# Reordering the opening of a two-layer trunk kernel: rope steps, input copies, loads, and extra products on TensorE

## The reference, cut to what matters

```python
for l in range(DEPTH):
    h = rmsnorm(x, norm_g[l])
    proj = h @ w_in[l]
    (a_q, a_k, a_v, a_gate, b_u, b_v, b_gate,
     c_q, c_f, c_i, c_gate, merge) = jnp.split(proj, SPLIT_IDX, axis=-1)
    qa = rope(a_q.reshape(b_, s_, A_HEADS, A_HEAD_DIM), positions)
    ka = rope(a_k.reshape(b_, s_, A_KV_HEADS, A_HEAD_DIM), positions)
    out_a = sliding_window_attention(qa, ka, va, attn_sinks[l]) * jax.nn.silu(a_gate)
    ...
    y = jnp.sum(gates * mixed, axis=2) @ w_out[l]
    x = x + y
return rmsnorm(x, final_g)
```

## Time and profile before

| What | us |
|---|---|
| Median of 3 runs | 1032.23 |
| Lowest and highest run | 1032.17, 1032.27 |
| The profiled execution | 1032.96 |
| Its span on the core | 1031.1 |

### The profile page before, as it was taken

How to read it: one execution, slowest core, us unless ns; L and a number is a source line. 1 busy time by engine, 2 the same in 40 slices (tenths; PEclk the granted TensorE clock), 3 DMA queues, 4 the chain that set the end, 5 groups by cost and what they waited for, 6 DMA issues and landing times.

```text
span 1031.1 us, 15310 instructions
## 1 busy us (share of the span) xinstructions
PE 1013.6 (98%) x6388; PEld 854.8 (83%) x6388; DVE 640.6 (62%) x840; ACT 517.5 (50%) x804; POOL 287.8 (28%) x144
## 2 busy tenths in 40 slices
PE   7989999999999999999999999999999999999997
PEld 6869899888888888888888989988888888888876
DVE  6888865899543535445628689479983444444552
ACT  6855774766552332223456766577546233332333
POOL 1221113532421413233212111153243232322430
PEclk9989999999999999999999999999999999999999
DMA  6512221222123323224342222212232232323602
GB/s 219 154 63 82 84 68 57 82 82 83 62 63 102 111 90 106 82 82 129 117 133 82 83 83 84 63 61 83 83 102 61 82 103 82 102 84 100 203 2 81
DMA packets 93428, 94.71 MB, mean 92 GB/s; under 512 B 2272, under 2 KB 91568, under 8 KB 93360
## 3 DMA queue, kind: packets, MB, share of 16 engines
q1 hardware_dynamic: 93088, 93.60, 29.3%
q10 hardware_dynamic: 272, 0.14, 0.1%
HBM read 91.64 MB, written 2.10 MB: 91 GB/s over the span
## 4 chain that ended last, share of the span: by engine, by line
PE 93%; DVE 3%; ACT 1%; issue 1%; DMA 1%; ACTq 0%; DVEq 0%
PE pj L504 27%; PE pj L505 26%; PE pj L506 26%; PE mx L641 2%; PE mx L504 1%; PE mx L505 1%; PE mx L506 1%; PE mx L581 1%; PE mx L604 1%; PE mx L701 1%; PE mx L669 1%; PE mx L589 1%; DVE q_rot L1421 1%; PE mx L679 1%; PE mx L672 1%
## 5 line engine op out<-in xcount | busy, mean ns | idle before, releaser
L1161 POOL TENSOR_TENSOR w_lo<-w_raw,w_hi 128x1024 fp32r<-128x1024 f32 (+1 forms) x89 | 196.3, 2206 | 571.6 <-ACT w_hi L818 571.3
L504 PE MATMUL pj<-h_hi,w_hi 128*128 128x512 f32 x832 | 330.2, 397 | 0.0
L506 PE MATMUL pj<-h_hi,w_lo 128*128 128x512 f32 x832 | 324.6, 390 | 0.0
L505 PE MATMUL pj<-h_lo,w_hi 128*128 128x512 f32 x832 | 324.5, 390 | 0.0
L818 ACT ACTIVATE w_hi<-w_raw 128x1024 fp32r<-128x1024 f32 (+1 forms) x179 | 159.1, 938 | 161.3 <-PE pj L506 161.1
L1271 DVE TENSOR_TENSOR w_lo<-w_raw,w_hi 128x1024 fp32r<-128x1024 f32 (+1 forms) x90 | 161.3, 1792 | 70.7 <-ACT w_hi L818 70.4
L504 PEld LDWEIGHTS pj<-h_hi,w_hi 128*128 128x128 f32 x832 | 156.6, 188 | 34.7 <-issue 3.0
L506 PEld LDWEIGHTS pj<-h_hi,w_lo 128*128 128x128 f32 x832 | 156.5, 188 | 33.0
L505 PEld LDWEIGHTS pj<-h_lo,w_hi 128*128 128x128 f32 x832 | 156.7, 188 | 32.1 <-issue 1.0
L1385 DVE TENSOR_TENSOR merge_gate<-pj,rstd 128x512 f32<-128x512 f32 x48 | 33.2, 691 | 162.9 <-PE pj L506 162.9
L936 ACT ACTIVATE merge_gate<-merge_gate,small 128x512 f32<-128x512 f32 x48 | 34.3, 715 | 89.3 <-DVE merge_gate L1385 89.3
(11 more groups left out here) (257 smaller groups left out, 1497.6 us busy)
## 6 DMA issues: line engine op xcount, KB each, us to landing
w_raw<-in_w_in SPq DMA_DIRECT2D x61, 1024.0 KB, 5.5
w_raw<-in_w_branch SPq DMA_DIRECT2D x24, 512.0 KB, 3.4
w_raw<-in_w_out SPq DMA_DIRECT2D x6, 1024.0 KB, 5.2
x_tokens<-in_x SPq DMA_DIRECT2D x4, 512.0 KB, 6.6
w_raw_last<-in_w_out SPq DMA_DIRECT2D x2, 1024.0 KB, 7.7
sp_w_rows<-in_sp_w SPq DMA_DIRECT2D x2, 512.0 KB, 6.4
out<-out_low SPq DMA_DIRECT2D x4, 256.0 KB, 2.0
out<-out_high SPq DMA_DIRECT2D x4, 256.0 KB, 2.3
```

The costliest lines, as they stand in the source:

```text
L504: pe.matmul(bank, wh, ah, start=first, stop=False)
L505: pe.matmul(bank, wh, al, start=False, stop=False)
L506: return pe.matmul(bank, wl, ah, start=False, stop=final)
L1161: return pool.tensor_tensor(out=dst, in0=full, in1=hi.bitcast(f32), op=ALU.subtract)
```

## The change

It touches layer 0 alone, and seven places. The ropes of layer 0 move from phases 3, 4, 4, 5, 6 to 3, 3, 4, 4, 5, and `values_even` from phase 5 to phase 6. TensorE gets four 128 x 128 products of a matrix of ones ahead of the gains' transpose and five behind it. The constants are loaded by SP, as its first transfer, and no longer by ACT. SP loads unit 1 ahead of the positions. ACT makes the high parts of blocks 6 and 7 ahead of the plain copies of blocks 2 to 5, and copies in the order 5, 2, 3, then the high part of unit 1, then 4, 6, 7. TensorE waits for five copies instead of six ahead of job 2.

```diff
-ROPE_FIRST = (3, 4, 4, 5, 6)
+ROPE_FIRST = (3, 3, 4, 4, 5)
...
             buf, src = unit_load(0)
+            sp.dma_start(CST[:, :], consts[:, :]).then_inc(cst_in, 16)
             load_x(0)
...
             load_x(3)
+            load_weights(sp, 1)
             sp.dma_start(POSI[:, :], positions[0].partition_broadcast(P)).then_inc(pos_in, 16)
-            for v in range(1, RB):
-                load_weights(sp, v)
+            load_weights(sp, 2)
...
+            def warm(count):
+                for _ in range(count):
+                    pe.matmul(M[0][:, 0:P], ONE[:, :], ONE[:, :], start=True, stop=True)
+
+            pe.wait_ge(fill_done, 1)
+            warm(4)
             pe.wait_ge(cst_in, 16)
             pe.wait_ge(norm_in, 16)
             pe.transpose(M[1][:, 0:16], VN[0:16, :], CST[0:16, 0:16]).then_inc(normT_done, 1)
+            warm(5)
             transpose_x(0)
...
-                        pe.wait_ge(xT_evac, 6)
+                        pe.wait_ge(xT_evac, 5)
...
-            act.dma_start(CST[:, :], consts[:, :]).then_inc(cst_in, 16)
...
             first_h(5)
+            first_h(6)
+            first_h(7)
+            x_evac(5)
             x_evac(2)
             x_evac(3)
-            first_h(6)
-            first_h(7)
+            split_hi(1)
             x_evac(4)
-            x_evac(5)
-            split_hi(1)
             x_evac(6)
             x_evac(7)
...
-                phase[V_JOB + 4].append((values_even,))
+                phase[V_JOB + (4 if layer else 5)].append((values_even,))
```

## The result

The changed kernel takes 1025.89 us (median of 4 runs, 1025.44 to 1027.41) against 1032.2: a ratio of 0.9941, 95% interval 0.9928 to 0.9954. That is 6.3 us faster. It lies in the range of 1023.4 to 1026.8, 1.6 us above the forecast of 1024.3 and next to the two rivals at 1026.1 and 1026.3.

The account below looks back on a forecast made before the run. TensorE was taken to bound the kernel, losing 6.93 us around its wait for the ropes ahead of layer 0's `scores(0)`. -6.93 - 1.05 (opening) = -8.0 us, 1032.23 to 1024.3 us; range 1023.4 to 1026.8.

Parts of the forecast that it names:

- the two rivals at 1026.1 and 1026.3: rival 1 (opening's clock stays low, 1026.1, 32%) and rival 3 (the wait moves, 1026.3, 6%).
- The ropes: Layer 0 ahead of `scores(0)`: ropes done at about 57.1, TensorE's wait and the clock's fall go, -6.9 us.
- What is late next: DVE behind the ropes: `neg_max(0)` at 63.5, unit 5's low part at 71.6, job 10 wanting it at 72.0; cost 0 to 1 us.
- My signs of being wrong: A wait over 0.5 us at job 6, 8 or 10, rope 4 ending after 59, or x's transposes starting after 7.
- The opening: Ahead of job 2: products raise the clock by job 0, job 2 starts 1.05 us earlier; 0.85 later with the clock low.
- rival 3: `scores(0)`, or job 10 for unit 5's low part, waits up to 2 us, too short for a clock fall: 1026.3, 6%.
- rival 4: DVE's unit 5 low part holds job 10; clock falls from 2.8 us of waiting on; slower than before, 2%.
- The sum: Whole kernel, clock up: -6.93 - 1.05 = -8.0 us; profiled execution 1025.0, median 1024.3, own range 1023.4 to 1025.4.
- rival 1: Opening: clock stays low until job 0 has run, opening loses 0.85 us, total -6.1, 1026.1; 32%.
- The copies: Opening: three ACT copies instead of two ahead of unit 1 make its low part 0.55 us later; relaxed wait worth nothing.
- The rule on transposes: TensorE's clock in the opening: transposes don't count as busy, so the products alone must raise it; its sum is rival 1's.

Follow-up runs that it names:

- experiment 3: The changed kernel with layer 0's ten `bounds` steps behind `neg_max(0)` on DVE instead of ahead of it: 1023.49 us (0.992).
- experiment 1: The kernel before with only the moves of layer 0's ropes and `values_even`, the opening as before: 1026.11 us (0.9942).
- experiment 8: The changed kernel with ACT's copies in the old order and TensorE waiting for six ahead of job 2: 1025.54 us (0.994).
- experiment 10: The kernel of experiment 3 with ACT's copies in the old order: 1023.48 us (0.9922).
- experiment 4: The changed kernel without the nine products of ones: 1026.51 us (0.9944).
- experiment 6: The kernel of experiment 3 without the nine products of ones: 1025.25 us (0.9934).
- experiment 2: The changed kernel with ropes and `values_even` where they were, so the opening's edits alone: 1030.86 us (0.9989).
- experiment 9: The kernel before with the rope part and the `bounds` steps behind `neg_max(0)`, the opening as before: 1024.96 us (0.9936).
- experiment 5: The changed kernel with the four products ahead of the gains' transpose, without the five behind it: 1027.74 us (0.9956).
- experiment 7: The kernel of experiment 3 with x's second slice issued ahead of the first piece of unit 0: 1024.41 us (0.9924).
- experiment 11: The kernel of experiment 10 with x's second slice issued ahead of the first piece of unit 0: 1023.6 us (0.9924).

## Why the prediction was right, and where it was off

**The ropes: right.** Rope 1 filled DVE's wait, rope 4 was held once by POOL, as rope 3 had been, and the ropes ended at 57.65 (said: 57.1, ahead of TensorE). The wait and the fall of the clock behind it went together. With the wait gone the term is 19.30 - 12.37 = 6.93 us, and experiment 3 shows 12.37 in its trace. The long operation was the third of rope 4 (54.16) and not the fourth, as I had it, which changes nothing.

**What is late next: the step that failed.** I put `neg_max(0)` at 63.5 and unit 5's low part at 71.6, and costed this at nothing, up to 1 us. `neg_max(0)` came at 65.10 and the low part at 71.99 to 73.2; TensorE lost 1.25 us up to the transposes and 0.4 at job 10. I had added up DVE's operations with the durations that they had before. But `bounds` had run at 64.5, after POOL's subtraction (60.38 to 63.21 then), and was moved to 60.3, into it. In these traces POOL follows ACT, and ACT's high part of unit 5 (59.00, before 59.24) follows the end of job 7, whose last matmul is at 58.51 (before 58.76). The 2 us are one operation of 128 x 4: without them `neg_max(0)` would have started at 63.0, close to my 63.5. I had used this very effect for rope 4 and for unit 1's low part and not looked for it here. The row shows the hold-up, in the changed kernel and in experiment 1; experiment 3 shows that both waits go once the steps stand behind `neg_max(0)`, but it takes their own 2.0 us away as well.

My signs of being wrong missed it. They named waits at jobs 6, 8 and 10 of over 0.5 us, and the larger wait stood at the transposes of the probabilities. Of what I had said the profile would show, four things did not come: 12.4 us from job 7 to the product behind job 9 (13.62), 0.13 us for each transpose of blocks 2 and 3 (0.25), job 2 at 23.8 (24.58), and unit 5's low part starting before 71 (71.99).

**The opening: mis-sized in this trace.** The term was -1.05. In the profiled execution job 2 starts 0.3 us earlier. The medians say -0.2 beside the ropes (experiment 1 and the result), -1.2 alone, -1.5 with bounds later, and only the second of these is clear of no change. The gains landed at 2.7, sooner than my lower bound of 3.9. The transposes started at 5.4, not 6.2, and the clock was up by then (1.10 us for the first eight), so the products did what they are there for. What I had not foreseen is that blocks 2 and 3 would then wait for the second slice of x, that this slice would land 1.1 us later than before (0.4 of it because the constants now stand ahead in SP's list), and that the clock would fall in that wait: job 2 started at 24.58, not 23.8. Under rivals 3 and 4 I had held a wait of 2 us too short for a fall and let it come at 2.8. Here it came at about 8.4, some 1.6 us into a wait that began at 6.8.

**The sum.** For the profiled execution I had 1025.0 and it took 1027.41: the 2.4 us are the 1.6 of the new waits and the 0.8 of the opening. The medians miss by only 1.6, since the profiled execution is 1.5 us above the median of its kernel, and that of before was 0.7 above. So a wait like rival 3's came about, with 1.6 of its 2 us, mostly at a place that it didn't name, and rival 1 gave nearly the right number for a wrong reason: the clock had risen. That the median lies in the range is in part luck: the upper end was drawn for these two rivals, and the forecast's own range ended at 1025.4.

**The copies.** Unit 1's low part was moved by 0.5 us as said, but neither experiment 8 nor 10 shows a time for it that can be told from zero.

**The rule on transposes.** I cited the Trainium skill's page TensorE: Matmul & The Clock Gate, Part 4, for transposes not counting for the clock. Experiment 4 speaks against it: the clock rose with transposes only. The kernel before had 4 us of them without a rise, and so had experiment 6, but experiment 1 shows that the moment differs by 2.3 us between executions of the same instructions; so that one trace didn't bear the rule out. The measurement decides.

**What stays open.** Why the second slice of x lands late. It took 6.5 to 6.7 us from issue in four traces with the five products behind the gains' transpose (the changed kernel, experiments 2, 3 and 8) and 5.5 to 5.7 in the three without them (4 to 6), but 5.8 in experiment 10, which has them. In the three traces with the old opening, which has no products but another order of transfers, it took 6.0 to 6.2. Products and a late slice go together, mostly; that one makes the other is not shown. Nor is the cause of the spread of 1 to 2 us between runs. The traces place it ahead of job 2, where two things are seen to differ: when x's slices land, and when the clock rises or falls.

## What to carry to other kernels

When a wait on one engine is taken away, everything that used to lie after it moves, and the engines beside it don't all move with it. Look at which operations of VectorE with two inputs in SBUF now meet a GpSimd subtraction: in these traces they cost what was left of it, down to one of 128 x 4 elements. Putting the ten small steps behind others that read PSUM gave 1.6 us in the traces and 2.4 in the medians. And when you bring up a cold TensorE ahead of its data, look at the next wait too: it took the clock back in two of the five traces with nine products and the old order of loads, and in a third the clock fell just behind it.

## What the runs showed of the hardware

- A VectorE operation of 128 x 4 elements lasted 2.23 us beside a GpSimd subtraction and 0.15 us without it. In its place beside the same subtraction, two operations that read PSUM (1.29 for both), memsets (0.19) and a maximum over PSUM (1.29 for two, as without POOL) were not slowed (experiment 3).
- The clock of TensorE rose at 13.9, 11.6 and 12.5 us in three executions with the same opening (before, experiments 1 and 9), from the first of the transposes at 5.9 to 6.2 on. It fell in a wait for x that began at 6.8 in the changed kernel (2.26 us) and in the same wait of experiment 3 (2.36), and stayed up through one of 2.25 us in experiment 2. In experiment 8 it fell at about 9.5, 0.6 us after a wait of 1.75 us had ended. In the kernel before it fell 2.6 us into the wait ahead of `scores(0)`.
- In experiment 4 it rose with transposes alone, at about 9.4; in experiment 6, with the same opening, at about 11.7. Four products that were followed by a wait of 1.9 us didn't (experiment 5); nine, the last of them right ahead of the transposes, brought it up by the end of the first eight transposes in each trace that has them (1.08 to 1.29 us for the eight with the old order of loads; 1.43 and 1.83 in experiments 7 and 11, where it rose among them).
- The norm gains landed 2.0 us after issue as the first transfer of their queue, and 4.4 us as the second, behind 96 KB of constants and beside the first slice of x.
